# Attention bias rows of a dilated-attention layer: from GpSimd's DMA queue to ScalarE's

## The reference

```python
# for each of 3 groups (rate 1, 4, 16), 16 heads of 64
steps = ql + Bk - kl
bucket = t5_bucket(jnp.maximum(steps, 0) * rate)
bias = bias_table[bucket].transpose(2, 0, 1)
...
s = jnp.einsum('brnqhd,brnkhd->brnhqk', qb, kk) * (dh ** -0.5) + bias
s = jnp.where(valid, s, NEG_INF)
m = jnp.max(s, axis=-1)
p = jnp.exp(s - m[..., None])
```

## Time and profile before

| | us |
|---|---|
| three timed runs | 1390.75, 1394.68, 1396.14 (median 1394.68) |
| profiled execution: time | 1390.73 |
| profiled execution: span of the profile | 1388.8 |
| TensorE busy in the span | 1070.0 (77%) |
| VectorE, ScalarE, GpSimd busy | 439.9, 343.3, 67.8 |

### The profile page before, as it was taken

The page is one execution under the profiler, slowest core; times in us unless marked ns, Lnnn a source line. Parts: engine busy times, 40 slices in busy tenths (PEclk is TensorE's granted clock), DMA queues, the critical chain, the costliest instruction groups (busy, mean ns, idle before and its releaser), DMA issues.

```text
span 1388.8 us, 15986 instructions
## 1 busy us (share of the span) xinstructions
PE 1070.0 (77%) x6816; PEld 626.1 (45%) x6816; DVE 439.9 (32%) x863; ACT 343.3 (25%) x563; POOL 67.8 (5%) x124
## 2 busy tenths in 40 slices
PE   8999999855756656587999998999766646565586
PEld 8987885321212212133888876776322212122131
DVE  6745536010000100003866665755110100101001
ACT  4334524100101001013555555543100001000010
POOL 2000000000000000000300015400000000000000
PEclk9999999987878898799999999999988878788888
DMA  9656689999999999999655656599999999999998
GB/s 350 231 182 238 223 337 410 415 428 428 426 429 428 426 427 427 428 422 390 169 186 182 243 178 134 143 352 429 428 428 427 428 428 428 428 427 428 428 423 323
DMA packets 75881, 489.02 MB, mean 352 GB/s; under 512 B 6176, under 2 KB 6416, under 8 KB 51232
## 3 DMA queue, kind: packets, MB, share of 16 engines
q1 hardware_dynamic: 71296, 480.53, 85.3%
q0 software_dynamic: 4096, 7.37, 2.9%
q10 hardware_dynamic: 416, 0.07, 0.0%
HBM read 486.77 MB, written 1.17 MB: 351 GB/s over the span
## 4 chain that ended last, share of the span: by engine, by line
DMA 49%; PE 39%; DVE 3%; SPq 3%; issue 2%; POOL 2%; ACT 2%; DVEq 0%; ACTq 0%
DMA ring<-in_exp_up 45%; PE quad L1424 9%; PE quad L381 8%; PE quad L383 7%; PE quad L382 7%; DMA ring<-in_dil_wq 1%; POOL work L2285 1%; DMA ring<-in_ret_w_in 1%; PE quad L1385 1%; DMA ring_more<-in_exp_down 1%; SPq L1038 1%; SPq L1044 1%; PE bank L1778 1%; POOL work L2289 1%; SPq L1056 1%
## 5 line engine op out<-in xcount | busy, mean ns | idle before, releaser
L1424 PE MATMUL quad<-ring,work 128*32 128x512 f32 x896 | 183.4, 708 | 91.5 <-DMA ring<-in_exp_up 91.5
L1443 PE MATMUL quad<-ring,work 128*32 128x512 f32 x512 | 133.6, 728 | 116.2 <-DMA ring_more<-in_exp_down 105.3
L1424 PE MATMUL quad<-ring_more,work 128*32 128x512 f32 x784 | 178.3, 680 | 58.1 <-DMA ring<-in_exp_gate 21.1
L1578 DVE TENSOR_TENSOR work<-work,quad 128x512 f32<-128x512 f32 x16 | 11.0, 687 | 480.5 <-PE quad L1424 421.1
L1424 PEld LDWEIGHTS quad<-ring,work 128*32 128x32 f32 x896 | 47.9, 128 | 181.0 <-issue 181.0
L1443 PE MATMUL quad<-ring_more,work 128*32 128x512 f32 x384 | 128.3, 696 | 0.3 <-DMA ring_more<-in_exp_down 0.3
L1587 DVE TENSOR_TENSOR h<-h,bank 128x512 f32<-128x512 f32 x64 | 44.0, 688 | 263.6 <-PE bank L1494 263.6
L1443 PEld LDWEIGHTS quad<-ring,work 128*32 128x32 f32 x512 | 34.6, 131 | 201.9 <-issue 200.1
L1424 PEld LDWEIGHTS quad<-ring_more,work 128*32 128x32 f32 x784 | 45.3, 123 | 122.7 <-issue 105.2
L363 DVE TENSOR_TENSOR lo_b<-ring,hi_b 128x2048 fp32r<-128x2048 f32 (+1 forms) x40 | 86.3, 2181 | 17.1 <-ACT hi_b L357 17.1
L1513 ACT ACTIVATE work<-bank,gains 128x128 f32<-128x128 f32 x128 | 36.9, 367 | 220.5 <-PE bank L1333 220.5
(11 more groups left out here) (341 smaller groups left out, 1833.7 us busy)
## 6 DMA issues: line engine op xcount, KB each, us to landing
ring<-in_exp_up SPq DMA_DIRECT2D x48, 2048.0 KB, 37.2
ring_more<-in_exp_gate SPq DMA_DIRECT2D x40, 2048.0 KB, 33.1
ring<-in_exp_down SPq DMA_DIRECT2D x32, 2048.0 KB, 35.1
ring_more<-in_exp_down SPq DMA_DIRECT2D x21, 2048.0 KB, 44.4
ring<-in_exp_gate SPq DMA_DIRECT2D x16, 2048.0 KB, 41.4
ring_more<-in_exp_up SPq DMA_DIRECT2D x16, 2048.0 KB, 40.1
ring<-in_w_kv SPq DMA_DIRECT2D x12, 2048.0 KB, 8.9
ring<-in_ret_w_in SPq DMA_DIRECT2D x11, 2048.0 KB, 10.6
```

The lines of the kernel that those rows point to most:

```text
L1424: last = nc.tensor.matmul(bank[2 + kind][rows, :], m_x[:, k, rows], w[e][:, kk * FF:(kk + 1) * FF], start=(k == 0), stop=(k == KD - 1))
L1443: last = nc.tensor.matmul(bank[4 + nh][rows, :], m_hidT[:, k * P + e * SLOTS:k * P + (e + 1) * SLOTS], w[e][:, at:at + 512], start=(k == 0 ...
```

## The change

The 12 DMAs a pair on GpSimd's queue become 8 on ScalarE's: the two `near` blocks of one head and side go in one DMA. Pairs 0 and 1 are loaded after ScalarE's weight splits in units 1 and 3 of the projections; pair `pr + 2` is loaded after `exps(pr, 1)` and ahead of `high` and `keep_v`. GpSimd loads no more in this part.

```diff
+        def load_bias(engine, pr):
+
+            for odd in range(2):
+                hd = 2 * pr + odd
+                for side in range(2):
+                    rows = slice(side * PER_CLASS, (side + 1) * PER_CLASS)
+                    near = bass.AP(bias_rows.tensor, hd * BW + side, [[CLASSES, PER_CLASS], [2, TT], [1, S]])
+                    at = bias_at[hd % 4]
+                    both = work[rows, at:at + TT * 3 * P].rearrange("p (t s) -> p t s", t=TT)[:, :, 0:S]
+                    engine.dma_start(both, near).then_inc(b_loaded[pr % 2], 16)
+                    own = bass.AP(bias_rows.tensor, (DIL_H + hd) * BW + NEAR_W,
+                                  [[1, PER_CLASS], [DIL_H * BW, 2], [1, PER_CLASS]])
+                    engine.dma_start(d_bias(hd)[rows, S:S + P].rearrange("p (g u) -> p g u", g=2), own
+                                     ).then_inc(b_loaded[pr % 2], 16)
...
                     split_next(split_act, act, FIRST_QKV + qk_tile(u), FIRST_QKV + v_tile(0))
+                    if u // 2 < 2:
+                        load_bias(act, u // 2)
...
                     exps(pr, 1)
+                if 0 <= pr < PAIRS - 2:
+                    load_bias(act, pr + 2)
                 if 0 <= pr - 3 < LATE:
                     high(pr - 3)
...
-            pool.wait_ge(b_stored, 16)
-            pool.wait_ge(q_done, 1)
-            for pr in range(PAIRS):
-                if pr >= 2:
-                    pool.wait_ge(a_sum, 4 * (pr - 1))
...
-                            pool.dma_start(d_bias(hd)[rows, t * 3 * P:t * 3 * P + S], near
-                                           ).then_inc(b_loaded[pr % 2], 16)
...
-                        pool.dma_start(d_bias(hd)[rows, S:S + P].rearrange("p (g u) -> p g u", g=2), own
-                                       ).then_inc(b_loaded[pr % 2], 16)
```

More of the change, by code:

```diff
@@ L1662, in build @@
         TABLES = 16 * 8
+        BIAS_LOADS = 2 * 2 * 2
         b_done = sem("bias_rows_made")
@@ L1974, in dilated_pe @@
                 wo_step(s)
+        def load_bias(engine, pr):
[11 more added lines that the diff above has]
+                                     ).then_inc(b_loaded[pr % 2], 16)
         def dilated_act(act):
             act.wait_ge(s_tables, TABLES)
+            act.wait_ge(b_stored, 16)
             def keep(u):
@@ L2120, in biased @@
                 if t == 0:
-                    dve.wait_ge(b_loaded[pr % 2], 16 * 12 * (pr // 2 + 1))
+                    dve.wait_ge(b_loaded[pr % 2], 16 * BIAS_LOADS * (pr // 2 + 1))
                     if pr >= 2:
@@ L2273, in _ @@
             route_loads(1)
-            pool.wait_ge(b_stored, 16)
-            pool.wait_ge(q_done, 1)
-            for pr in range(PAIRS):
-                if pr >= 2:
-                    pool.wait_ge(a_sum, 4 * (pr - 1))
[L2279 to L2284, removed]
-                            pool.dma_start(d_bias(hd)[rows, t * 3 * P:t * 3 * P + S], near
-                                           ).then_inc(b_loaded[pr % 2], 16)
-                        own = bass.AP(bias_rows.tensor, (DIL_H + hd) * BW + NEAR_W,
-                                      [[1, PER_CLASS], [DIL_H * BW, 2], [1, PER_CLASS]])
-                        pool.dma_start(d_bias(hd)[rows, S:S + P].rearrange("p (g u) -> p g u", g=2), own
-                                       ).then_inc(b_loaded[pr % 2], 16)
         @block.scalar
```

## The result

| | before | after |
|---|---|---|
| median of four runs, us | 1394.37 | 1408.18 |
| lowest and highest, us | 1390.75, 1396.14 | 1405.26, 1410.90 |
| span of the profiled execution, us | 1388.8 | 1408.1 |
| TensorE, VectorE, ScalarE, GpSimd busy, us | 1070.0, 439.9, 343.3, 67.8 | 1072.3, 439.6, 343.7, 15.5 |

The changed kernel is slower: 1.012 times the time of before, 95% interval 1.0098 to 1.0141. The prediction gave 1390.2 us with a range up to 1401, so it is wrong in sign and range. What it called rival 2 (an issue on ScalarE costs 0.6 us or more, 1403 us) is what came.

The account below looks back on a forecast made before the run. TensorE's stops in attention, behind late bias rows from GpSimd, delay the DMA-bound expert stream one for one. 1390.73 - 8.5 gained + 4.0 cost = 1386.2 us; against the median 1390.2 us, range 1384 to 1401.

Parts of the forecast that it names:

- rival 2: Slower: an issue on ScalarE costs 0.6 us or more, 17 us lost against 8.5 gained, so 1403 us; chance 0.16.
- The gain, 8.5 us: TensorE's stops ahead of `scores(2, 1)` and `scores(5, 1)` go, with half clock: 3.78 + 1.60 + 1.56 + 1.58 us.
- rival 3: Bias rows still land late, stops stay by half and ScalarE's cost comes on top: no change, about 1394.7; chance 0.08.
- I take 3.0: Eight issues on ScalarE take 3.6 us, 0.6 beside the last exponential, so its other work is held 3.0 us.
- Pair 0: TensorE stands 1.82 us ahead of `turned(0, 2)` (3.0 held less 1.18 slack), plus 1.57 half clock: 3.4 us cost.
- Pair 1: `keep_turned(1, 0)` ends at 843.3, TensorE, already 3.4 us late, wants it at 843.2: 0.1 us cost.
- Pair 2, "I count nothing": From pair 2's turn `values` lengthens TensorE's turn, giving ScalarE room: no cost counted.
- Pairs 3 to 5: Loads delay `high`, so VectorE's `low` and `biased` come 0.4, 1.05 and 0.2 us late; 0.55 slack leaves 0.5 us cost.
- The early loads: Loads of pairs 0 and 1 in the projections, covered by VectorE's split and the norm: nothing counted, up to 1 us uncovered.
- One microsecond of attention is one of the whole: The expert stream starts only when attention frees ring slots, so attention's gain or loss moves the end one for one.
- Rival 1: Issues cost nothing, made while ScalarE stands 2.74 us for row minima: full 8.5 us won, 1386.2 against the median; chance 0.26.
- The rule weighed against the rows: Sequencer free only once descriptors are made; shared, locked generator would make ScalarE's issue wait up to SyncE's row each meeting.

Follow-up runs that it names:

- the eight-unread kernel: Against the change: real loads on SyncE, ScalarE issues eight plain unread 128x16 DMAs a pair at the change's place; 1401.87 us, ratio 1.008 to before.
- the two forms: Real loads on SyncE, eight unread DMAs a pair added on ScalarE: plain 128x16 (1401.87 us) or 64 partitions x 2 blocks like the change's loads (1411.67 us).
- the twelve: Against the change: loads at the same places on ScalarE's queue but unmerged, 12 DMAs a pair; 1430.9 us, ratio 1.0291 to before.
- the four-unread kernel: Against the change: real loads on SyncE, ScalarE issues four plain unread 128x16 DMAs a pair at the change's place; 1386.35 us, ratio 0.9965 to before.

## Why the prediction was wrong, step by step

- **The gain, 8.5 us: right.** Both stops and the half clock behind them are gone, and with the loads on SyncE the span falls by 8.5 us, the median by 7.0. The rows are in time: VectorE waits for none (rival 3 falls).
- **"I take 3.0": the step that failed.** The hold was worked out as eight times the spacing of the two issues in the earlier trace rows, 0.45 us. It measured 4.44 to 7.31 us. In its quietest burst (from 874.03 us) the change's first issue takes 0.52 us and each of the other seven 0.62 to 0.63; in the burst of pair 2, just behind a tile that SyncE issued, they go up to 1.93. In the plain form of 16 columns the price of the earlier trace rows does hold at this place, for two issues (0.35, 0.45) and in a quiet burst for most of eight (hold 3.40 us). So the rows were read rightly and stretched too far: two DMAs of other forms, with no tile ahead of them, don't price eight of this one. The bound of 3.6 us was no bound either (at that hold the prediction's own steps give 0.8 us for pair 1, not 0.5; that changes nothing). The overlap of 0.6 us with the last exponential was right.
- **Pair 0: right in mechanism, size off.** The hold less the slack is 7.31 - 1.18 = 6.1; TensorE stands 6.23 us, at the place forecast, with half clock behind.
- **Pair 1**, 0.1 forecast, 2.39 measured. By the prediction's own steps: the copy comes 6.2 us (TensorE's delay) and 4.9 us (hold) later, at 837.91 + 0.59 + 11.1 = 849.6; TensorE wants it at 839.77 + 6.2 + 1.57 = 847.5, so 2.1 us. Size again.
- **Pair 2, "I count nothing": a missed wait.** I looked only for `turned`. The first `values` needs the last `keep_v`, which the diff's order rows show behind the eight issues; 4.33 us and half clock at 0.57 over 4 us, some 6 us. Moving the loads behind `keep_v` removes this stop. Even with the hold right, rival 2's sum of 17 us leaves it out.
- **Pairs 3 to 5**, 0.5 forecast: a second missed path. `low` waits 5.5 us at the longest for `high`, where "some 3 us longer" was forecast. But by the forecast path, over VectorE to `scores`, come only 0.63 and 0.45 us of TensorE's stops; 1.16, 0.86 and 1.95 us stand ahead of `turned(pr - 1, 2)`, for ScalarE's own copy, which the prediction followed in pairs 0 and 1 alone. With the half clock (1.4 and 2.1 us) that is 8.5 us. Rival 2 has 8.5 for these pairs too, by the other path: luck.
- **The early loads, nothing: right.** ScalarE stands 1.85 and 1.60 us for them in the change, and the cover named hides it.
- **One microsecond of attention is one of the whole: right.** An expert tile is issued 18.9 us later, the span grew by 19.3, and the stream kept its rate.
- **Rival 1 falls.** In 2.75 us of ScalarE's standing no issue was made. The rule of the Trainium skill's page "Perfetto Trace Analysis", section "DVE / Act Engine Instruction", that a sequencer is ready for the next instruction once one is in the wait queue, would have put them there; the trace does not agree for issues behind exponentials that still wait (row minimum until 826.00, issue at 826.05, last exponential at 826.06). The program could not have used such a gain either: `load_bias` waits for nothing itself, and an issue ahead of that row minimum could have overwritten biases that VectorE still read.
- **The rule weighed against the rows** (a generator shared with SyncE, locked by one at a time; the Trainium skill, "Perfetto Trace Analysis", section "DMA Instruction — HWDGE (DVE, Sync)"). Its other part, that a sequencer is free only after the issue, shows in the change: the last issue of pair 2 ends at 834.02 us, and ScalarE's next instruction starts at 834.07. The earlier trace rows had not shown it, since the start there is put down to PEq. As to the lock: in the burst from 874.03 us, with no issue of SyncE's between 858 and 886, the first takes 0.52 us and each of the other seven 0.62 to 0.63. So 0.62 is the price without a meeting, and the loss needs none. Nor do the dearer ones (0.8 to 1.93) need one: SyncE's issue ahead of pair 2's burst lasts 0.54 us and is over at 825.97, before the burst, and with all loads on SyncE and none on ScalarE single issues take up to 1.30 us as well. Where both engines issue at once, in the eight-unread kernel from 839.66 to 842.21 us, SyncE's take the 0.60 to 0.61 us that they also take with none on ScalarE:

```profile
840.96 0.60 SPq L1990 DMA_DIRECT2D work<-bias_rows  x1
841.03 0.62 ACTq L2004 DMA_DIRECT2D unread<-shape_constants  x1
```

So no wait of one engine for the other's issue shows there. Right behind (842.25 and 842.34) both have a dear one at the same time, 1.36 and 1.27 us. Nine of the change's eleven dearer issues stand in bursts beside or just behind a tile that SyncE issued; what makes them dear stays open.
- **The chances.** Rival 2 turned at 0.50 us an issue and had 0.16, on the strength of two rows, while SyncE's rows had a median of 1.5 us. The nearer engine outweighed the nearer situation (several in a row, tiles in flight).

The hold decides over the whole series: 0.2 us cost nothing, 1.2 to 1.9 cost 2.8 us, 3.4 to 4.8 cost 18.3, 4.8 to 6.9 cost 28.1, 6.9 to 9.7 cost 47.3 (each against the loads on SyncE). That fits a turn where the hold passes the slack of 1.18 us, which the prediction had read rightly; no kernel has holds between 0.5 and 1.2.

Open: why an issue of the change's form takes 0.62 us and single ones much more, how much of the 1.2 us between the two forms (median holds 4.5 and 5.7) comes from meeting SyncE's issues, and what makes GpSimd pause for 7 to 8 us.

## What to carry to other kernels

DMA issues are work of the engine that issues them: price a burst from a burst of DMAs of the same form, with the same tiles in flight, not from a lone pair, and follow every instruction queued behind it, each to its first reader, not only to the one on the path so far. Put issues ahead of a wait that the engine has anyway, in twos and fours, or on an engine with nothing queued behind. A stop of TensorE here cost about half as much again through its clock, so a few long holds are dearer than the sum of their idle time.

## What the runs showed of the hardware

- Issues in a row on ScalarE in attention: the first mostly 0.33 to 0.35 us (plain, 16 columns), 0.45 to 0.46 (plain, 256 columns) or 0.52 (two blocks). Later ones in bursts away from a tile's issue take mostly 0.45 to 0.64 us (plain, 16 columns) or 0.61 to 0.64 (the change and the twelve), with single ones of 1.0 to 1.3. Behind the issue of a 2 MB tile they go up to 1.93 (2.24 in the twelve). The Trainium skill's page "DMA: Bandwidth & Descriptors", section "Issuing engines are not separate DMA queues", calls the sequencer's time to start a DMA usually small beside the DMA itself. The trace agrees for one DMA (0.62 us of issue, 3.7 us to landing, medians of the change), but issues of a burst add up on the engine: the eight of pair 2 took 8.0 us (826.05 to 834.07).
- Behind the stops of 1.95, 2.39, 4.33 and 6.23 us in the change, and behind 1.60 in the earlier trace rows, TensorE ran at half clock for some time; behind one of 1.91 us in the four-unread kernel it didn't (granted clock 1.00 from 820 to 930 us).
- GpSimd's pause lasted from 831.4 to 838.3 us behind ten loads of pair 2, and from 830.4 to 838.2 behind seven merged ones. The number of loads issued doesn't set it.
